# Splitting weights in quarters of a unit, with VectorE's part a quarter behind ScalarE's

## The reference

```python
for i in range(4):
    h = rms_norm(x, norm_mix_g[i])
    mix = (fourier_mixer, s5_mixer, dilated_attention_mixer, fourier_mixer)[i](h, ...)
    x = x + mix
    h = rms_norm(x, norm_ffn_g[i])
    gate, up = split(h @ w_gate_up)          # 1024 x 5632
    x = x + (silu(gate) * up) @ w_down       # 2816 x 1024
```

## Time and profile before

| | us |
|---|---|
| three timed runs | 3061.48, 3066.1, 3074.41; median 3066.1 |
| span of the profiled execution | 3075.9 |
| TensorE busy (PE) | 92% |
| VectorE (DVE) / ScalarE (ACT) / GpSimd (POOL) busy | 51% / 36% / 10% |
| DMA traffic | 304.81 MB, mean 99 GB/s |

### The profile page before, as it was taken

One profiled execution on the slowest core, in us unless ns is written; L12 is line 12 of the kernel. 1 busy time (PEld: TensorE's weight loads), 2 busy tenths in 40 slices (PEclk: granted clock), 3 DMA queues, 4 the chain that ended last, 5 costly groups with the idle time before them and its releaser, 6 DMA issues. The chain is left out here.

```text
span 3075.9 us, 38003 instructions
## 1 busy us (share of the span) xinstructions
PE 2820.2 (92%) x15338; PEld 2273.3 (74%) x15338; DVE 1562.1 (51%) x2299; ACT 1121.1 (36%) x1724; POOL 313.2 (10%) x262
## 2 busy tenths in 40 slices
PE   5999997579999989989999799999799999888887
PEld 5878886567888867768788578888688888666665
DVE  5776664754433442554535654344544344554665
ACT  4332332263322322754647332122332122532442
POOL 2333221010000000111102300000200000110000
PEclk9999999789999999989999899999899999999888
DMA  3244545533444223113232322222122222211101
GB/s 106 89 147 155 164 146 179 217 124 106 127 123 123 96 69 110 69 50 105 77 113 86 134 82 96 96 97 95 41 96 96 96 96 96 78 42 42 40 15 43
DMA packets 115264, 304.81 MB, mean 99 GB/s; under 512 B 28320, under 2 KB 73824, under 8 KB 86288
## 3 DMA queue, kind: packets, MB, share of 16 engines
q1 hardware_dynamic: 109968, 280.88, 28.0%
q10 hardware_dynamic: 5120, 21.50, 1.9%
HBM read 264.68 MB, written 41.85 MB: 100 GB/s over the span
## 5 line engine op out<-in xcount | busy, mean ns | idle before, releaser
L94 PE MATMUL ps<-hh_,wh_ 128*128 128x512 f32 x2184 | 872.1, 399 | 19.5 <-DVE hl_ L121 11.3
L94 PE MATMUL ps<-hl_,wh_ 128*128 128x512 f32 x2184 | 858.1, 393 | 0.0
L94 PE MATMUL ps<-hh_,wl_ 128*128 128x512 f32 x2184 | 857.4, 393 | 0.0
L121 DVE TENSOR_TENSOR wl_<-raw_,wh_ 128x2048 fp32r<-128x2048 f32 (+2 forms) x213 | 480.8, 2257 | 544.3 <-ACT wh_ L117 544.2
L117 ACT ACTIVATE wh_<-raw_ 128x2048 fp32r<-128x2048 f32 (+2 forms) x213 | 400.0, 1878 | 369.9 <-PE ps L94 347.6
L94 PEld LDWEIGHTS ps<-hh_,wh_ 128*128 128x128 f32 x2184 | 414.3, 190 | 122.0 <-DVE hl_ L121 10.2
L94 PEld LDWEIGHTS ps<-hh_,wl_ 128*128 128x128 f32 x2184 | 414.6, 190 | 88.4
L94 PEld LDWEIGHTS ps<-hl_,wh_ 128*128 128x128 f32 x2184 | 415.0, 190 | 86.5 <-issue 2.8
L94 PE MATMUL ps<-ah_,wl_ 128*128 128x512 f32 x704 | 279.5, 397 | 0.0
L94 PE MATMUL ps<-ah_,wh_ 128*128 128x512 f32 x704 | 278.3, 395 | 0.0
L94 PE MATMUL ps<-al_,wh_ 128*128 128x512 f32 x704 | 277.7, 395 | 0.0
(11 more groups left out here) (345 smaller groups left out, 3527.3 us busy)
## 6 DMA issues: line engine op xcount, KB each, us to landing
raw_<-in_w SPq DMA_DIRECT2D x205, 1024.0 KB, 4.9
sO<-s5ce_ SPq DMA_DIRECT2D x32, 256.0 KB, 4.1
sW<-s5wt_ SPq DMA_DIRECT2D x16, 512.0 KB, 3.7
sA<-os_ SPq DMA_DIRECT2D x24, 256.0 KB, 2.2
ol_<-sA SPq DMA_DIRECT2D x24, 256.0 KB, 3.7
sT<-sK SPq DMA_DIRECT2D x32, 128.0 KB, 3.3
wh_<-sO ACTq DMA_DIRECT2D x4, 1024.0 KB, 13.6
wl_<-sO ACTq DMA_DIRECT2D x4, 1024.0 KB, 15.2
```

Of the source, the lines that this page charges most:

```text
L94: return self.e.matmul(out, lhsT, rhs, start=start, stop=stop, skip_group_check=True)
L121: return Nothing() if self.e is None else self.e.tensor_tensor(out, a, b, op)
```

## The change

ScalarE makes the high part of unit u+2 in quarters of 512 columns, at tiles 0, 4, 8 and 12 of unit u. VectorE makes the low part one quarter behind: at tile 0 it makes only the last quarter of unit u+1, and at tiles 4, 8 and 12 quarters 1, 2 and 3 of unit u+2. The count of finished quarters is kept for each engine (`staged`). A call that covers several of these places at once takes the quarters in one instruction for each unit (`highs(K, ac, 8)`: 1024 columns; `lows(K, dv, 16)`: the last quarter of unit u+1, then 1536 columns of unit u+2). Direct calls of `high` and `low` still ask for whole units, and finish what is left of the unit before first. The split units stay whole. The semaphore values for `hi` are kept by quarter, and the low part waits for its own quarters only; TensorE still waits for `lo`, which is the last quarter. `load` and `loads` are unchanged.

```diff
+def pieces(K, e, upto, parts):
+
+    end = min(4 * upto + parts, 4 * e.upto + 4)
+    while e.staged < end:
+        u, a = e.staged // 4, e.staged % 4
+        b = 4 if u in K.split else min(4, end - 4 * u)
+        e.staged = 4 * u + b
+        yield u, a, b, slice(0, width(K, u)) if u in K.split else slice(512 * a, 512 * b)
+
+
+def high(K, ac, upto, parts=4):
+    for u, a, b, s in pieces(K, ac, upto, parts):
         ac.wait_ge(*K.at("raw", u))
         if u >= SLOTS:
             ac.wait_ge(*K.at("used", u - SLOTS))
-        n = width(K, u)
-        ac.act(K.wh[K.slot[u]][:, 0:n], K.raw[u % RAWS][:, 0:n], ACT.Copy).then_inc(*ac.up("hi", u))
-        ac.staged += 1
+        ac.act(K.wh[K.slot[u]][:, s], K.raw[u % RAWS][:, s], ACT.Copy).then_inc(*ac.up())
+        for q in range(a, b):
+            ac.mark("hi", u, q)
 
-def low(K, dv, upto):
-    while dv.staged <= min(upto, dv.upto):
-        u = dv.staged
+def low(K, dv, upto, parts=4):
+    for u, a, b, s in pieces(K, dv, upto, parts):
         t = K.slot[u]
-        dv.wait_ge(*K.at("hi", u))
-        n = width(K, u)
-        dv.tt(K.wl[t][:, 0:n], K.raw[u % RAWS][:, 0:n], K.wh[t][:, 0:n].bitcast(F32), ALU.subtract).then_inc(*dv.up("lo", u))
-        dv.staged += 1
+        dv.wait_ge(*K.at("hi", u, b - 1))
+        dv.tt(K.wl[t][:, s], K.raw[u % RAWS][:, s], K.wh[t][:, s].bitcast(F32), ALU.subtract).then_inc(
+            *dv.up(*(("lo", u) if b == 4 else ())))
 
 def highs(K, ac, n):
-    for u, j in ac.tiles(n):
-        if j == 0:
-            high(K, ac, u + 2)
+    at = [(u, j // 4) for u, j in ac.tiles(n) if j % 4 == 0]
+    if at:
+        high(K, ac, at[-1][0] + 2, at[-1][1] + 1)
 
 def lows(K, dv, n):
-    for u, j in dv.tiles(n):
-        if j == 0:
-            low(K, dv, u + 2)
+
+    at = [(u, j // 4) for u, j in dv.tiles(n) if j % 4 == 0]
+    if at:
+        low(K, dv, at[-1][0] + 2, at[-1][1])
```

More of the change, by code:

```diff
@@ L274, in load @@
         sp.staged += 1
-def high(K, ac, upto):
-    while ac.staged <= min(upto, ac.upto):
-        u = ac.staged
+def pieces(K, e, upto, parts):
[7 more added lines that the diff above has]
+    for u, a, b, s in pieces(K, ac, upto, parts):
         ac.wait_ge(*K.at("raw", u))
```

## The result

| | median us | runs | ratio to before, 95% interval |
|---|---|---|---|
| before | 3066.4 | 3061.5 to 3074.4, 4 runs | |
| changed | 3089.6 | 3086.9 to 3091.0, 4 runs | 1.0063 (1.0047 to 1.0078) |
| both again, another chip (e10) | 3090.4; before 3066.0 | 6 and 14 runs | 1.0069 (1.0053 to 1.0085) |

The change makes the kernel slower by 0.6 to 0.7%, 23 us in the medians. The forecast was 3075 us with a range of 3050 to 3095: the time lies inside, but near the rival in which the lag becomes a wait in each head pair (3095 us). The profiled execution has a span of 3085.0 us, only 9.1 above that of before; a second trace of before (e0) has 3070.8, 5 us less.

What follows compares the result with a forecast made beforehand. The prediction took TensorE to bound the kernel, busy 2820 of 3076 us. Losses of 22.5 us less gains of 14 made +8.5 us on the median of 3066.1: 3075 us, range 3050 to 3095.

Steps and rivals of the forecast that it cites:

- the rival in which the lag becomes a wait in each head pair: Attention: VectorE's 1536-column part waits for ScalarE's last quarter, delaying `qk_`; 12 to 40 us, about 3095 us, chance 0.21.
- FFNs pay nothing: Gated FFNs: the closing quarter comes 11 us ahead of its use, added instructions cost nothing; 366 us as before.
- (b): Attention, group 0 to group 1: TensorE waits for the closing quarter behind VectorE's softmax; 7 to 12 us lost, taken 10.
- (c): Attention, group 1 to group 2: TensorE waits for the closing quarter behind VectorE's `qk_` step; 2 to 7 us, taken 5.5.
- (a): Start of attention: values matmuls wait for the closing quarter behind VectorE's norm steps; 0.8 to 3 us lost, taken 2.
- (d): Mixing after attention: `ol_` loads queue on SP behind a load awaiting the late closing quarter; -6 to +6 us, taken +4.
- (e): Head pairs 1 in attention: VectorE waits for ScalarE's fourth quarter, `qk_` just makes the scores; 0 to 2 us, taken 1.
- Mixers 12, ends 5 and 17: Last layer's mixers: shorter blocks on the chain give back 14.7 us less 3; gain taken 12, ends 5 and 17.
- the 3 us deducted for added instructions on the chain: Last layer's mixers: about five additional quarters of 0.6 us fall on the chain elsewhere in the stretch, 3 us off the gain.
- S5 tables 2: First FFN: TensorE's 2.47 us idle for `s5wn_` can go with VectorE in quarters; gain 0 to 2.5 us, taken 2.
- The chain of waits holds "almost none" of the splitting before 2600 us: Reading of the profile: the chain of waits holds almost no splitting steps before 2600 us, and six places behind that.
- a sum outside +5 to +12 in the stretches: Sign of failure: the forecast is wrong if the four stretches' changes don't sum to +5 to +12 us.

Runs made afterwards that it cites:

- e10: The changed kernel again with no edit, on another chip: 3090.4 us against 3066.0 before, ratio 1.0069.
- e0: The kernel before again with no edit, for a second trace: one run of 3072.6 us, span 3070.8.
- e4: The changed kernel with ScalarE making whole units again and only VectorE in quarters: 3080.5 us against 3072.0 before, ratio 1.0029.
- e8: The changed kernel with quarters only in the first 38 units and from unit 189 on, whole units between: 3048.5 us against 3066.0 before, ratio 0.9939.
- e6: The changed kernel with whole units while TensorE works on units 114 to 118 (last head pair and mixing after attention): one run, 3086.3 us.
- e9: The changed kernel with halves of 1024 columns, only in the first 38 units and from unit 189 on: 3060.0 us against 3066.0 before, ratio 0.9968.
- e2: The changed kernel with quarters only from unit 189 on (last layer's mixers), whole units elsewhere: 3052.8 us against 3072.7 before, ratio 0.9930.
- e3: The changed kernel with quarters only at units 78 to 118 (attention and the mixing behind it), whole units elsewhere: 3111.2 us, ratio 1.0124 to before.
- e1: The changed kernel with whole units at units 78 to 118 (attention and the mixing behind it): 3053.3 us against 3072.7 before, ratio 0.9932.

## Why the prediction was right, and where it was wrong

- *FFNs pay nothing*: right, 366.00 us as before.
- *(b) 10 and (c) 5.5 us*: right, 9.5 and 5.5 in e4. TensorE idled 9.92 and 3.62 us for `wl_`.
- *(a) 2*: 2.0 to 3.4 in the traces with the lag there, of which up to 1.5 can be before's own spread (e0 and e8 have 1.5 and 1.6 with whole units). The wait is the one forecast, 5.11 us for `wl_`; its size is right as far as it can be told.
- *(d) +4*: right in sign and path, 4 to 6.5; SP's queue is what carries the delay, as e6 shows.
- *(e) 1, ends 0 and 2*: the step that failed. I checked the scores, the reader of `qk_`, and found 0.1 to 0.9 us of slack. But `qk_` also frees a bank for which the transposes wait one step ahead of the scores. That costs 0.9 us for each pair in group 0 and 0.3 to 0.7 in the others, 15 us in all (changed less e4: 7.8 + 4.0 + 3.3). It is the rival of the head pairs: VectorE behind ScalarE's last quarter and `qk_` behind VectorE, as written, priced 12 to 40, and 15 came. The place is another. The forecast looked for waits of the scores (`ps<-qk_`) in many pairs; TensorE's matmuls there wait in three (one in before), and the weight loads of the transposes in fifteen.
- *Mixers 12, ends 5 and 17*: 18 came, just above the high end. The places hold, laid on before: 2702 and 2723 had 4.2 between them and give 4.7 to 6.1 from 2690 to 2750 (against the one or the other trace of before); 2811 had 6.7 with the clock and gives 6.6; 2881 had 1.3 and gives 1.4. Against the 3 us deducted for added instructions on the chain, 1.2 (at 2930) is the most that shows at one place, and the last 65 us gave 2.7 for which I had no term. Part of the gain is the clock: after the idle of 5.03 us at 2811.04 the clock was at half for 10 us; that idle is gone, and the stretch now has 0.84.
- *S5 tables 2*: right, the 2.4 to 2.5 us of idle went in each trace with quarters in the first FFN, and from 120 to 480 us these traces are 1.9 to 2.6 us shorter (e9, with halves, 1.2; e0, e2 and e3 0). GpSimd's step went from 3.08 to 1.49 us with quarters and 2.03 with halves on VectorE, which agrees with the rule of the Trainium skill that the forecast weighed ("SBUF — State Buffer", Who interferes with whom).
- *The chain of waits holds "almost none" of the splitting before 2600 us*: misread. That chain starts at 1799.6 us; it never covered attention, where all that went wrong lies. The slack in the head pairs was read from single pairs in order of time, and only for the scores.

Sum of the terms as measured: 3 + 9.5 + 5.5 + 15 + 5 = 38 lost, 18 + 2.4 = 20 gained: +18, where the forecast had 22.5 and 14: +8.5. Two errors of 15 and 6 with opposite signs, and the larger one decides. The forecast named a sum outside +5 to +12 in the stretches as the sign that it is wrong, and +18 is outside. That the time still lies within the range is no merit of the forecast's sum: the upper end was set at the rival's mean, and the gains came out 6 us larger than their term. The medians are 23 to 24 us apart, 5 to 6 more than the traces account for; before's own runs spread by as much. The rule on breaking instructions up (the Trainium skill, "Perfetto Trace Analysis", Optimizing Scalar/DVE Operations) is borne out by e8, but only in stages with bubbles: where the pieces bring a wait for the other engine's last piece, as in the head pairs, they make bubbles.

## What to carry to other kernels

When a step is delayed, follow every consumer of everything behind it on its engine: the reader of its result, and also whoever waits for the buffer or bank that it frees. Merged pieces of a producer in two halves make the consumer wait for the second half, ahead of all other work in its queue. Splitting a preparation step finely pays in stretches of small chained steps and costs where a merged piece makes an in-order engine wait; where TensorE sets the pace with a lead to spare it does neither. So choose it by stage (e1, e2 and e8, all 17 to 20 us below before), not for the kernel as a whole.

Before a chain of waits is said to hold nothing of a kind, look where it starts. And look for waits of TensorE in its weight loads: the matmul row showed less than half of this one.

## What the runs showed of the hardware

VectorE's 512 columns took 0.69 us in a trace full of them (0.68 forecast) and ScalarE's 0.62; halves took 1.23 and 1.05 (e9). A stretch of before between the same VectorE instructions took 30.0 us at a granted clock of 0.83 in one trace and 26.2 at 0.99 in another (e0). Where TensorE waited for `qk_`, its weight loads showed 15.4 us of added idle and its matmuls 6.4; the pairs got 15.1 us longer. The same program has runs 10 us apart while the granted clock of the core moves from 0.959 to 0.954, while ten runs of the change lie within 5 us (3086.9 to 3091.6); what makes the difference wasn't tried.
